# The fourth layer's delta rule by chunks of 64 tokens in tiles half as wide, with products in quarters of the array

## The reference, cut to what matters

```python
qkv = jax.nn.silu(causal_dwconv(proj[..., :GDN_QKV_W], conv_w))
q = l2norm(q.reshape(B, S, GDN_HEADS, GDN_DK))
k = l2norm(k.reshape(B, S, GDN_HEADS, GDN_DK))
...
a = jnp.where(strict, jnp.einsum('nbhid,nbhjd->nbhij', k_beta, kc) * decay, 0.0)
t_mat = lax.linalg.triangular_solve(a + eye, ...)      # inverse of a 64 x 64 unit triangle per chunk and head
w_val = t_mat @ v_beta
k_cum = t_mat @ (k_beta * jnp.exp(gc)[..., None])
attn = jnp.einsum('nbhid,nbhjd->nbhij', qc, kc) * decay

def step(state, xs):
    q_i, kc_i, w_i, at_i, ke_i, dl_i = xs
    v_new = w_i - jnp.einsum('bhcd,bhdv->bhcv', kc_i, state)
    o_i = jnp.einsum('bhcd,bhdv->bhcv', q_i, state) + jnp.einsum('bhij,bhjv->bhiv', at_i, v_new)
    state = state * dl_i[..., None, None] + jnp.einsum('bhcd,bhcv->bhdv', ke_i, v_new)
    return state, o_i
o = gated_rmsnorm(o, gate.reshape(B, S, GDN_HEADS, GDN_DV), o_norm)
```

## Time and profile before

| | |
|---|---|
| median of 3 timed runs | 3168.7 us (3168.34 to 3177.97) |
| profiled execution | 3162.18 us, span 3160.9 us |
| mean granted TensorE clock | 0.967 |
| busy | PE 2919.8 us (92%), PEld 2079.9, DVE 1179.3 (37%), ACT 480.9 (15%), POOL 102.7 (3%) |
| chain that ended last | PE 79%, DMA 10%, DVE 6%, ACT 2% |
| HBM | 703.6 MB read, 224 GB/s over the span |

### The profile page before, as it was taken

One profiled execution on the slowest core, in us unless ns is written; L12 is line 12 of the kernel. 1 busy time (PEld: TensorE's weight loads), 2 busy tenths in 40 slices (PEclk: granted clock), 3 DMA queues, 4 the chain that ended last, 5 costly groups with the idle time before them and its releaser, 6 DMA issues.

```text
span 3160.9 us, 40792 instructions
## 1 busy us (share of the span) xinstructions
PE 2919.8 (92%) x15750; PEld 2079.9 (66%) x15750; DVE 1179.3 (37%) x2588; ACT 480.9 (15%) x1051; POOL 102.7 (3%) x98
## 2 busy tenths in 40 slices
PE   7998899999998899999999999998968789999998
PEld 5666678787666688887755555556868665555554
DVE  2435324433435324442344222225475244222223
ACT  2222301001222311001211111111310111111111
POOL 0000000000000000000010000000000001000000
PEclk9998899999998899999999999999979889999999
DMA  5222146563222146654459999993300229999995
GB/s 186 77 80 74 60 143 242 201 250 106 80 80 80 54 161 240 251 208 157 165 215 395 404 401 400 410 401 139 133 14 1 111 116 409 398 405 404 392 394 228
DMA packets 104979, 684.59 MB, mean 217 GB/s; under 512 B 17760, under 2 KB 19312, under 8 KB 24496
## 3 DMA queue, kind: packets, MB, share of 16 engines
q1 hardware_dynamic: 93040, 665.22, 53.6%
q0 software_dynamic: 11264, 16.54, 1.5%
q10 hardware_dynamic: 576, 1.43, 0.1%
HBM read 703.57 MB, written 4.19 MB: 224 GB/s over the span
## 4 chain that ended last, share of the span: by engine, by line
PE 79%; DMA 10%; DVE 6%; ACT 2%; issue 1%; SPq 0%; DVEq 0%; ACTq 0%; POOLq 0%
PE PS L454 75%; DMA wmoe<-in_experts 10%; PE PS L459 4%; ACT AR L2114 1%; DMA COLS<-in_cols 0%; ACT AR L2164 0%; SPq L2663 0%; DVE wmoe L1826 0%; DVE H L1826 0%; DMA AR<-tokens,IX 0%; ACT ST L2114 0%; DVE ST L1304 0%; DVE wmoe L1324 0%; ACT wmoe L2114 0%; DVE wmoe L1834 0%
## 5 line engine op out<-in xcount | busy, mean ns | idle before, releaser
L454 PE MATMUL PS<-wmoe,AR 128*64 128x256 f32 (+1 forms) x5360 | 716.0, 423 | 33.4 <-DMA wmoe<-in_experts 22.1
L454 PE MATMUL PS<-H,wdense 128*128 128x256 f32 (+1 forms) x3056 | 713.8, 394 | 9.1 <-DVE H L1334 3.6
L454 PEld LDWEIGHTS PS<-H,wdense 128*128 128x128 f32 x3056 | 587.0, 194 | 119.3 <-issue 15.1
L454 PEld LDWEIGHTS PS<-wmoe,AR 128*64 128x64 f32 x5360 | 384.2, 137 | 317.2 <-issue 142.3
L2114 ACT ACTIVATE AR<-PS 128x256 f32<-128x256 f32 (+4 forms) x512 | 231.9, 457 | 1706.6 <-PE PS L454 1100.9
L454 PE MATMUL PS<-AR,wdense 128*128 128x256 f32 (+1 forms) x1920 | 440.4, 389 | 28.9 <-DVE AR L1864 9.8
L454 PE MATMUL PS<-AR 128*128 128x512 f32 (+13 forms) x1492 | 401.4, 408 | 48.3 <-DVE AR L1311 13.8
L454 PEld LDWEIGHTS PS<-AR,wdense 128*128 128x128 f32 x1920 | 367.3, 192 | 95.8 <-issue 20.4
L454 PEld LDWEIGHTS PS<-AR 128*128 128x128 f32 (+6 forms) x1492 | 209.1, 189 | 147.7 <-issue 90.5
L459 PEld LDWEIGHTS PS<-CST,AR 128*128 128x128 f32 (+5 forms) x1158 | 131.8, 135 | 167.1 <-issue 137.8
L454 PE MATMUL PS<-wdense,H 128*128 128x256 f32 (+4 forms) x1024 | 219.7, 371 | 0.0
(11 more groups left out here) (286 smaller groups left out, 1541.6 us busy)
## 6 DMA issues: line engine op xcount, KB each, us to landing
wmoe<-in_experts SPq DMA_DIRECT2D x402, 1024.0 KB, 8.8
wdense<-in_dense SPq DMA_DIRECT2D x176, 1024.0 KB, 4.8
...
AR<-tokens,IX POOLq DMA_INDIRECT x71, 7.8
```

What stands on the lines that cost most here:

```text
L454: return te.matmul(out, lhsT, rhs, start=start, stop=stop, skip_group_check=True)
```

## The change

- All tiles of the inversion, and XX, BB, AM, TI, TT and the masked product of k and q (`QK`, before in DT), hold only the blocks on the diagonal: [128, 8, 64], the first chunk of a tile on partitions 0 to 63 and the second on 64 to 127. GB, KBG, VB, KEND, KCT and VN stay 128 wide.
- `by_chunk` makes their products: for each head one on rows and columns 0 to 63 of the array and one on 64 to 127, 16 of 64 x 64 x 64, all into one bank. The running sum, and beta, spread over columns, come from the same helper with a stationary operand broadcast from one column, without `RW`.
- Level 0 is I minus AM and I minus its transpose, so five levels with products are left, the last without "ti".
- In a chunk TT x VB and KCT x state are apart; kv and the output use 64 rows; the first chunk leaves out the state, the last kv. The norm's squares, sums and products are done chunk by chunk, and the sigmoid and the gate's product ahead of the chunks.
- `odd_order` sets one order for all engines: ba first, all qkv outputs with the norms of q and k between the last ones, then the gate, the preparation, v, gate product, chunks with the norm between them. `O_RAW` has four buffers and lies in wmoe. ACT copies every gate output (before DVE and ACT in turn).
- SP waits for the last "odd o" instead of the last state. The table of constants is 384 columns smaller, and the dense weights of ba lie ahead of those of qkv.

The diff, cut to its core:

```diff
-    c["strictT"] = same & (i[:, None] < i[None])
     lev = []
     for s in range(6):
         b = 1 << s
         lev.append((i[:, None] // (2 * b) == i[None] // (2 * b)) & (i[:, None] % (2 * b) < b) & (i[None] % (2 * b) >= b))
-    c["levelT"] = np.concatenate(lev, 1)
+    by_chunk = lambda m: np.concatenate([m[:CH, :CH], m[CH:, CH:]])
+    c["levelT"] = np.concatenate([by_chunk(m) for m in lev], 1)
+    c["chunk_cum"], c["chunk_ident"] = by_chunk(c["cum"]), by_chunk(c["ident"])
...
-    parts += wide("od_w_in_2", 0, 0, 16) + wide("od_w_in_2", 0, 4096, 1, step=16) + wide("od_w_out_2", 0, 0, 4)
+    parts += wide("od_w_in_2", 0, 4096, 1, step=16) + wide("od_w_in_2", 0, 0, 16) + wide("od_w_out_2", 0, 0, 4)
...
+    def odd_order(ba, qkv, silu, qk, p0, p1, v0, v1, gate, gated, chunks, out):
+
+        return in_turn((ba, 2), (qkv, 4), (silu, 1), (qkv, 1), (silu, 1), (qkv, 3), (silu, 1), (qkv, 1), (silu, 1), (qkv, 3), (silu, 1),
+                       (qkv, 1), (silu, 1), (qkv, 3), (silu, 1), (qkv, 1), (silu, 1), (qk, 1), (qkv, 1), (qk, 3), (qkv, 1), (qk, 3),
+                       (qkv, 1), (qk, 3), (qkv, 1), (qk, 2), (qkv, 3), (silu, 4), (gate, 8),
+                       *[(p, 1) for _ in range(17) for p in (p0, p1)], (v0, 1), (v1, 1), (gated, 2),
+                       (chunks, 3), (out, 1), (chunks, 2), (out, 1), (chunks, 1), (out, 2), (chunks, 2), (out, 1), (chunks, 1), (out, 2),
+                       (chunks, 2), (out, 1), (chunks, 1), (out, 5))
...
-    O_RAW = [area(O_KEEP + j * (S + 3), S + 3) for j in range(2)]
...
-    O_BUF = [tiles_of(AR[:, O_KEEP:O_KEEP + 8 * DC * P], 8) + tiles_of(h_flat, 2), tiles_of(wm_flat, 10)]
+    O_RAW = [wm_flat[:, 10 * DC * P + j * (S + 3):10 * DC * P + (j + 1) * (S + 3)] for j in range(4)]
+    O_TILES = [AR[:, O_KEEP + j * DC * P:O_KEEP + (j + 1) * DC * P] for j in range(8)]
+    O_TILES += [wm_flat[:, j * DC * P:(j + 1) * DC * P] for j in range(10)]
+    O_SQ = [area(4096 + 512 * j, 8, CH) for j in range(2)]
+    CHUNKS = [(0, 0), (0, 1), (1, 0), (1, 1)]
...
         def odd_mixer():
-            steps = feature_steps(("odd qkv",), H, DC, S, 12, lambda j: AC, ("odd h",))
-            run(steps)
-            norms = norm_heads(("odd qk",), 4, [O_MIX[:, 0:4, :], O_MIX[:, 4:8, :]])
...
+            def by_chunk(what, lhs, rhs, *readers):
+
+                o = bank(what, *readers)
+                for j in range(8):
+                    for r0 in (0, CH):
+                        m = mm(o[r0:r0 + CH, j * CH:(j + 1) * CH], lhs(j, slice(r0, r0 + CH)), rhs(j, slice(r0, r0 + CH)))
+                PE.up(m, *what)
...
+                    for r in (slice(0, CH), slice(CH, P)):
+                        m = mm(o[r, j * CH:(j + 1) * CH], AM[r, j, :], ident[r, r])
+                PE.up(m, "am turned", t)
...
+                for s in range(1, 6):
+                    te.wait_ge(VE.sem, VE.of("ti", t, s - 1))
+                    by_chunk(("ax", t, s), lambda j, r: AM[r, j, :], lambda j, r: TI[r, j, :], AC)
+                    yield
+                    te.wait_ge(VE.sem, VE.of("tt", t, s - 1))
+                    te.wait_ge(AC.sem, AC.of("ax", t, s))
+                    if s < 5:
+                        by_chunk(("ti", t, s), lambda j, r: TT[r, j, :], lambda j, r: XX[r, j, :], VE)
+                    by_chunk(("tt", t, s), lambda j, r: XX[r, j, :], lambda j, r: TT[r, j, :], VE)
+                    yield
+                te.wait_ge(VE.sem, VE.of("tt", t, 5))
+                both = [bank(("kct", t, r), reader(r)) for r in range(2)]
+                for j in range(8):
+                    for r, rows in enumerate((slice(0, CH), slice(CH, P))):
+                        m = mm(both[r][:, j * CH:(j + 1) * CH], KBG[rows, j, :], TT[rows, j, :])
+                        if j == 7:
+                            PE.up(m, "kct", t, r)
+                yield
...
-                for s in range(6):
-                    yield
-                    te.wait_ge(VE.sem, VE.of("am", t, s))
-                    by_head("ax%d" % s, t, lambda j: AM[:, j, :], lambda j: TI[:, j, :], lambda q: reader(q))
-                    yield
-                    te.wait_ge(VE.sem, VE.of("ax%d" % s, t, 0))
-                    te.wait_ge(AC.sem, AC.of("ax%d" % s, t, 1))
-                    for q in range(2):
-                        o1, o2 = bank(("ti", t, s, q), VE), bank(("tt", t, s, q), VE)
-                        for h in range(4):
-                            j = 4 * q + h
-                            mm(o1[:, h * P:(h + 1) * P], TT[:, j, :], XX[:, j, :])
-                            m = mm(o2[:, h * P:(h + 1) * P], XX[:, j, :], TT[:, j, :])
-                        PE.up(m, "tt", t, s, q)
...
+            def chunks():
+                for n, (t, r) in enumerate(CHUNKS):
+                    GB, KBG, VB, KEND, KCT, VN, QK, BB, TI, TT, AM, XX = odd_tiles(t)
+                    rows, tok = slice(CH * r, CH * r + CH), slice(t * P + CH * r, t * P + CH * r + CH)
+                    te.wait_ge(VE.sem, VE.of("v turned", t, 1))
+                    vn = [bank(("vn", t, r, q), reader(q))[rows, :] for q in range(2)]
                     for j in range(8):
-                        mm(o[:, j * CH:(j + 1) * CH], O_STATE[:, j, :], O_QC[:, j, t * P + r0:t * P + r0 + CH], start=True, stop=False)
-                        m = mm(o[:, j * CH:(j + 1) * CH], VN[:, j, :], DT[:, j, r0:r0 + CH], start=False, stop=True)
+                        m = mm(vn[j // 4][:, (j % 4) * P:(j % 4 + 1) * P], TT[rows, j, :], VB[rows, j, :], start=j % 4 == 0, stop=n == 0)
+                        if n == 0 and j % 4 == 3:
+                            PE.up(m, "vn", t, r, j // 4)
+                    yield
+                    o = bank(("odd o", t, r), VE)
+                    if n > 0:
+                        te.wait_ge(VE.sem, VE.of("kct", t, 0))
+                        te.wait_ge(AC.sem, AC.of("kct", t, 1))
+                        te.wait_ge(VE.sem, VE.of("state", n - 1))
+                        for j in range(8):
+                            m = mm(vn[j // 4][:, (j % 4) * P:(j % 4 + 1) * P], KCT[:, j, rows], O_STATE[:, j, :], start=False, stop=True)
+                            if j % 4 == 3:
+                                PE.up(m, "vn", t, r, j // 4)
+                        for j in range(8):
+                            mm(o[:, j * CH:(j + 1) * CH], O_STATE[:, j, :], O_QC[:, j, tok], start=j == 0, stop=False)
+                    yield
+                    te.wait_ge(VE.sem, VE.of("vn", t, r, 0))
+                    if n < 3:
+                        kv = [bank(("kv", t, r, q), VE) for q in range(2)]
+                    for j in range(8):
+                        if j == 4:
+                            te.wait_ge(AC.sem, AC.of("vn", t, r, 1))
+                        if n < 3:
+                            m = mm(kv[j // 4][:, (j % 4) * P:(j % 4 + 1) * P], KEND[rows, j, :], VN[rows, j, :])
+                            if j % 4 == 3:
+                                PE.up(m, "kv", t, r, j // 4)
+                    for j in range(8):
+                        m = mm(o[:, j * CH:(j + 1) * CH], VN[rows, j, :], QK[rows, j, :], start=n == 0, stop=True)
                     PE.up(m, "odd o", t, r)
-                    os = [bank(("kv", t, r, q), VE) for q in range(2)]
-                    for j in range(8):
-                        m = mm(os[j // 4][:, (j % 4) * P:(j % 4 + 1) * P], KEND[r0:r0 + 64, j, :], VN[r0:r0 + 64, j, :])
-                    PE.up(m, "kv", t, r)
-            run(norm_heads(("odd",), 2, [O_MIX[:, 0:4, :], O_MIX[:, 4:8, :]]))
-            te.wait_ge(VE.sem, VE.of("odd mix"))
+                    yield
+
+            def out():
+                    te.wait_ge(AC.sem, AC.of("odd", "squared", n))
+                    o = bank(("odd", "sums", n), AC)
+                    PE.up(mm(o, ones, O_SQ[n % 2]), "odd", "sums", n)
...
+                ve.wait_ge(PE.sem, PE.of("gd", t))
+                VE.up(ve.tensor_tensor(XX, eight(ps("gd", t)), each, ALU.min), "gd", t)
+                own()
+                VE.up(ve.tensor_tensor(XX, XX, each, ALU.subtract), "dt log", t)
...
+                VE.up(ve.tensor_tensor(TT, every("chunk_ident"), AM, ALU.subtract), "tt", t, 0)
+                ve.wait_ge(PE.sem, PE.of("am turned", t))
+                own()
+                VE.up(ve.tensor_tensor(AM, BB, every("levelT", CH), ALU.mult), "am", t, 1)
+                VE.up(ve.tensor_tensor(TI, every("chunk_ident"), eight(ps("am turned", t)), ALU.subtract), "am turned", t)
+                VE.mark("ti", t, 0)
+                ve.wait_ge(AC.sem, AC.of("gb", t, 1))
+                VE.up(ve.tensor_tensor(O_QC[:, :, t * P:(t + 1) * P], O_QC[:, :, t * P:(t + 1) * P], GB, ALU.mult))
+                yield
+                for s in range(1, 6):
+                    if s < 5:
+                        ve.wait_ge(PE.sem, PE.of("ax", t, s))
+                        VE.up(ve.tensor_tensor(AM, BB, every("levelT", CH * (s + 1)), ALU.mult), "am", t, s + 1)
```

(37 more changed lines are left out.)

440 lines of the change are left out of this document (235 added, 205 removed).

## The result

The changed kernel takes **3075.3 us** (median of four runs, 3066.4 to 3087.5) beside 3168.5 us for the kernel before (four runs, 3166.0 to 3178.0): ratio 0.9703, 95% interval 0.9661 to 0.9745. The prediction was 3062, its range 3045 to 3100. The profiled execution took 3080.08 us, its span 3078.8.

The account below looks back on a forecast made before the run. TensorE, busy 92% of the span, was taken as the bound, so its waits and reducible work in the fourth layer's mixer counted. The terms started the output projection 107 us earlier: 3168.7 - 107 = 3062, range 3045 to 3100.

Parts of the forecast that it names:

- Projections, +3.0: Fourth layer's mixer projections: 3.0 us longer, from 1.6 us waiting at the 16-column product and 1.4 for a late first norm.
- Preparation, T+25.4: Preparation before the inversion levels: 25 us instead of 55, paced by VectorE's operations on tiles half as wide.
- Levels to T+51: Inversion levels 1 to 5: 26 us instead of 76, products in quarters running two at once, 0.80 us each.
- KCT 4.2: KCT products after the levels: 32 records per tile at 0.065 us each, 4.2 us.
- KCT's end to the first kv 8.3: Transposes, sigmoids and table loads before the chunks, ending with vn copied at T+63.5; TensorE waits 4 us.
- Chunks 33.5: The mixer's four chunks: 33 us instead of 58, 9.8 us of TensorE a chunk, 2.3 us for climbing clock.
- Norm and gate 4.1: After the last o: 4 us instead of 22, as three quarters of the norm lie in the chunks.
- V and the gate: Step between levels and chunks, priced with KCT at 12 us: transposes, sigmoids, table loads, reaching T+62.9.
- number 1: Rival: quarters run one after the other, 54 ns a record, a level 10.4 us of TensorE, total 3088; chance 12%.
- number 5: Rival: slower than before, each change of diagonal quarter waiting for the array to empty, +218 us, total 3280; chance 3%.
- Number 3: Rival: the sequencer limits records; at about 62 ns per matmul a level takes 12 us, total 3094; chance 3%.
- Rival 2: Half clock through the levels: a product 1.6 us, a level 9.6 us, KCT +3, total 3087; chance 10%.

Follow-up runs that it names:

- ba_second: The changed kernel with the 16-column product moved from first to second place among the projections; 3068.3 us, ratio 0.9682.
- rows128: The changed kernel with kv and o contracting over all 128 rows instead of 64, the other rows of VN zero; 3065.3 us, ratio 0.9663.
- changed_again: The changed kernel run once more, unedited; 3074.5 us, ratio 0.9712.
- serial: The changed kernel with products in quarters issuing eight heads of rows 0 to 63, then eight of rows 64 to 127, instead of alternating; 3127.5 us, ratio 0.9877.
- fill: The changed kernel with four useless 128-row products in TensorE's wait just before chunk 0's state product; 3074.8 us, ratio 0.9693.
- gate_early: The changed kernel with the gate's sigmoids, table loads and V moved into the preparation and VectorE's gate products between the levels; 3072.5 us, ratio 0.9699.
- prep_fill_again: Second run of the changed kernel with six useless products in TensorE's wait ahead of level 1; 3080.2 us, ratio 0.9711.

## Why the prediction was right, and where it was off

The time lies in the range that was stated, and the gain in the levels, the preparation and the norm came by the mechanisms as written. It is 13 us above the forecast, from one term above all, and there the mechanism was not as written. T, the end of the gates, is 2306.52 here.

- **Projections, +3.0: 128.02 instead of 122.39, +5.6.** The 16-column product at the front was priced at 1.6 us of waiting; it took 8.16 us there instead of 3.64: it waited for H column by column, then 22 of its records ran at half clock, and so did the first outputs behind it, to 2191. ba_second shows that the place did it: 4.0 of the 5.6 go when it stands second. The 1.4 us priced for a late first norm did not come: its sums follow the outputs without a gap (2251.31).
- **Preparation, T+25.4: T+25.7** (the second tile's first ax at 2332.19). The count of VectorE's operations gave it.
- **Levels to T+51: KCT starts at 2360.65, T+54.1.** A product is 0.95 us, not 0.80, a level 5.7, not 5.0. The 25 ns of the earlier trace rows came from a single group of 16 records; 29 to 31 hold over whole levels. Level 1 ran at half clock and took 7.5 us for 6.6.
- **KCT 4.2: 3.7. KCT's end to the first kv 8.3: 7.4**, with a wait of 3.47 us for the 4 predicted.
- **Chunks 33.5: 45.9.** This is the step that failed, a cost taken at the wrong clock. "Chunks: 33 us instead of 58" sized every record at the full-clock 0.11 us of the earlier trace rows and allowed the clock only 2.3 us, after the wait. But the clock of the earlier trace rows was 1.00 among other products; here 64-row products make most of each chunk (48 of its 82 records). The kernel before had 64-row products in its kv, 16 records at a time and at clock 1.00 (2429.46 to 2431.51); now kv, o and the next TT x VB put 48 in a row, and the clock fell to 0.50 under them with TensorE 45.90 of 45.90 us busy. With kv and o over 128 rows the same stretch took 34.86. Without pauses between chunks and with state and copies hidden, the rest of the step stands: 10.1 us from sums to sums in rows128 for the 9.8 predicted.
- **Norm and gate 4.1: 4.1.** The stretch after the output projection lost nothing (657.0 against 659.4 us), the experts' later transfers included.

2.6 + 0.3 + 2.8 - 0.5 - 0.9 + 12.4 add up to 16.7 of the 17 us that the mixer's gain fell short (89.9 for 107). How far off the chunks are depends on the execution: changed_again, the same kernel, took 39.0 us for them. The sum has one slip besides: the terms given for V and the gate add up to about T+61.7, and the T+62.9 beside them has 1.2 us more than any of them names.

Of the rivals, number 1 is refuted by 32 against 52 ns a record in quarters at 1.00, and number 5 with it. Number 3 would have needed a floor above 29 to 31 ns, at which records follow each other here. The Trainium skill gives about 62 ns for each matmul when decoding is left to microcode (TensorE: Matmul & The Clock Gate, "Wait — 56ns, not 53.3ns?"); these 29 to 31 ns show no such cost. The Trainium skill's rule that different row tiles can't access one PSUM bank at the same time (TensorEngine Tiling (Array Packing), "Gotcha 1: PSUM Pressure") is not borne out by these products: both row halves write one bank, into different partitions, and alternating them is 1.6 to 1.7 times as fast as not (32 against 52 ns). Rival 2 named the right kind of loss in the wrong place. The earlier trace rows showed it for 16 rows, and I set it aside because the levels use both halves of 64 rows. In the levels that was right; the chunks use one half at a time, and I didn't ask the same question there. The four profiles with 128 rows and serial show that this is the difference.

What stays open is when the clock falls under 64-row products: the same instructions held 1.00 in some chunks and not in others, and neither the wait ahead (fill and gate_early had none) nor the order (changed_again and prep_fill_again have the same in the chunks) explains which. Also open is which of kv, o and TT x VB it takes: rows128 left TT x VB at 64 rows, and the clock held.
